# One load into 128 partitions in place of two into 64, in the attention stage of an encoder block

## The reference

```python
# A: 8 query heads on 2 key heads of 64, rotary, window of 2 chunks of 64, a learned sink per head
scores = jnp.einsum('bnqkgd,bnskd->bnkgqs', qc, kb) * (HEAD_DIM ** -0.5)
...
# B: 8 heads of 64, own chunk and the 8 before it, learned relative bias
scores = jnp.einsum('bnqhd,bnshd->bnhqs', qc, kb) * (HEAD_DIM ** -0.5)
scores = scores + bias[None, None]
probs = jax.nn.softmax(scores, axis=-1)
out = jnp.einsum('bnhqs,bnshd->bnqhd', probs, vb)
```

## Time and profile before

| | us |
|---|---|
| median of three runs | 2660.44 (2657.34 to 2663.78) |
| the profiled execution | 2667.05, its span 2665.1 |
| attention stage in the profile | 855 to 1232 |
| TensorE busy in the whole span | 2340.2 (88%) |
| VectorE, ScalarE, GpSimd busy | 1274.5, 1021.4, 837.4 |
| moved by the DMA engines | 508.67 MB, mean 191 GB/s |

### The profile page before, as it was taken

One profiled execution on the slowest core, in us unless ns is written; L12 is line 12 of the kernel. 1 busy time (PEld: TensorE's weight loads), 2 busy tenths in 40 slices (PEclk: granted clock), 3 DMA queues, 4 the chain that ended last, 5 costly groups with the idle time before them and its releaser, 6 DMA issues. The chain is left out here.

```text
span 2665.1 us, 37120 instructions
## 1 busy us (share of the span) xinstructions
PE 2340.2 (88%) x12222; PEld 1989.5 (75%) x12223; DVE 1274.5 (48%) x1935; ACT 1021.4 (38%) x1761; POOL 837.4 (31%) x801
## 2 busy tenths in 40 slices
PE   3899998999997789893699999559999999999990
PEld 2688887788886678883699999448888888888870
DVE  7201111100000567774433333476865758797774
ACT  4211111111111567774221221144654646576653
POOL 4255665510000011111222222034433434354451
PEclk9999999999998899997899999669999999999995
DMA  4145566622112877754544443358877979799987
GB/s 151 56 147 161 196 197 191 186 99 71 71 63 84 200 190 173 188 130 134 183 147 148 149 141 121 128 187 282 309 251 217 318 237 335 244 369 328 318 265 270
DMA packets 231745, 508.67 MB, mean 191 GB/s; under 512 B 25457, under 2 KB 88305, under 8 KB 230513
## 3 DMA queue, kind: packets, MB, share of 16 engines
q1 hardware_dynamic: 158480, 341.95, 38.6%
q0 software_dynamic: 32032, 93.35, 14.1%
q10 hardware_dynamic: 41152, 72.37, 7.7%
HBM read 386.13 MB, written 121.44 MB: 190 GB/s over the span
## 5 line engine op out<-in xcount | busy, mean ns | idle before, releaser
L408 DVE TENSOR_TENSOR pj_w_lo<-pj_w_raw,pj_w_hi 128x1024 fp32r<-128x1024 f32 x38 | 53.9, 1420 | 619.6 <-ACT pj_w_hi L300 619.5
L459 PE MATMUL pj_bank<-pj_hT_hi,pj_w_hi 128*128 128x512 f32 x960 | 259.4, 392 | 9.1 <-DVE pj_f_lo L425 5.7
L300 ACT ACTIVATE pj_w_hi<-pj_w_raw 128x1024 fp32r<-128x1024 f32 x38 | 40.2, 1060 | 591.8 <-PE pj_bank L459 520.8
L459 PE MATMUL pj_bank<-pj_hT_lo,pj_w_hi 128*128 128x512 f32 x960 | 258.4, 391 | 0.0
L459 PE MATMUL pj_bank<-pj_hT_hi,pj_w_lo 128*128 128x512 f32 x960 | 258.4, 391 | 0.0
L1870 POOL TENSOR_TENSOR ex_wd_lo<-weights_raw_d,ex_wd_hi 128x1024 fp32r<-128x1024 f32 x64 | 191.5, 3013 | 131.3 <-ACT ex_wd_hi L1898 131.3
L459 PEld LDWEIGHTS pj_bank<-pj_hT_hi,pj_w_hi 128*128 128x128 f32 x960 | 181.9, 190 | 47.8 <-issue 6.1
L459 PEld LDWEIGHTS pj_bank<-pj_hT_hi,pj_w_lo 128*128 128x128 f32 x960 | 181.4, 189 | 37.9
L459 PEld LDWEIGHTS pj_bank<-pj_hT_lo,pj_w_hi 128*128 128x128 f32 x960 | 181.4, 189 | 37.8
L1476 PE MATMUL mg_y_ps<-mg_aT_hi,mg_w_hi 128*128 128x256 f32 x512 | 149.3, 292 | 56.3 <-DVE mg_aT_lo L1388 48.8
L1952 DVE TENSOR_TENSOR ex_wd_lo<-weights_raw_d,ex_wd_hi 128x1024 fp32r<-128x1024 f32 x64 | 163.7, 2597 | 10.5 <-ACT ex_wd_hi L1898 10.5
(11 more groups left out here) (273 smaller groups left out, 5745.2 us busy)
## 6 DMA issues: line engine op xcount, KB each, us to landing
weights_raw_g<-in_w_exp_gate_dram SPq DMA_DIRECT2D x128, 512.0 KB, 5.9
weights_raw_u<-in_w_exp_up_dram SPq DMA_DIRECT2D x128, 512.0 KB, 8.9
weights_raw_d<-in_w_exp_down_dram SPq DMA_DIRECT2D x128, 512.0 KB, 6.8
pj_w_raw<-in_w_feat_dram SPq DMA_DIRECT2D x38, 512.0 KB, 4.5
scratch_gates<-pj_f_hi ACTq DMA_DIRECT2D x32, 512.0 KB, 4.9
mg_g_in<-scratch_gates SPq DMA_DIRECT2D x128, 128.0 KB, 2.9
pj_x_in<-in_x_dram SPq DMA_DIRECT2D x16, 512.0 KB, 3.5
scratch_qk<-pj_f_hi ACTq DMA_DIRECT2D x16, 512.0 KB, 5.0
```

The costliest lines, as they stand in the source:

```text
L300: act.activation(w_hi[n % 2][:], w_raw[n % 2][:], ACT.Copy).then_inc(whi_done, 1)
L408: dve.tensor_tensor(w_lo[n % 2][:], w_raw[n % 2][:], w_hi[n % 2][:], ALU.subtract).then_inc(wlo_done, 1)
L459: last = pe.matmul(eight[4 * p + b][:], w[p][:, k * P:(k + 1) * P], h[:, k, b * NB:(b + 1) * NB], start=(k == 0 and n == 0), stop=(k == KD ...
```

## The change

Each pair of loads into the lower and the upper 64 partitions becomes one load into all 128. For `k_st` and `aq_st` the source pattern gets a first dimension over the two parts; for `q_hi`, `q_lo`, `ak_hi` and `ak_lo` it gets a first dimension of size 2 and step 0 (`broadcast_to`). The counts that TensorE waits for are halved. The bytes written are the same.

```diff
-        QK_LOADS = 6
+        QK_LOADS = 3
...
-                sp.dma_start(k_st[p][:DH, cols].bitcast(F32), qk[0, k, rows, cols]).then_inc(landed, 16)
-                sp.dma_start(k_st[p][DH:, cols].bitcast(F32), qk[1, k, rows, cols]).then_inc(landed, 16)
+                sp.dma_start(k_st[p][:, cols].bitcast(F32), qk[:, k, rows, cols]).then_inc(landed, 16)
                 for part, both in enumerate((q_hi, q_lo)):
-                    for low in range(2):
-                        sp.dma_start(both[p][low * DH:(low + 1) * DH, cols].bitcast(F32), qk[part, q, rows, cols]
-                                     ).then_inc(landed, 16)
+                    sp.dma_start(both[p][:, cols].bitcast(F32),
+                                 qk[part, q, rows, cols].unsqueeze(0).broadcast_to([2, DH, HALF])).then_inc(landed, 16)
...
                 for part, keys in enumerate((ak_hi, ak_lo)):
-                    for low in range(2):
-                        sp.dma_start(keys[low * DH:(low + 1) * DH, padded_cols].bitcast(F32), rot_k[part, rows, cols]
-                                     ).then_inc(ak_in[c], 16)
+                    sp.dma_start(keys[:, padded_cols].bitcast(F32),
+                                 rot_k[part, rows, cols].unsqueeze(0).broadcast_to([2, DH, K_COLS])).then_inc(ak_in[c], 16)
...
-                for part in range(2):
-                    sp.dma_start(aq_st[seg % 2][part * DH:(part + 1) * DH, :, :].bitcast(F32),
-                                 rot_q[part, g, :, first:first + SEG_WINDOWS, :, :].rearrange("d w h q -> d w (h q)")
-                                 ).then_inc(aq_in[seg % 2], 16)
+                sp.dma_start(aq_st[seg % 2][:].bitcast(F32).rearrange("p w n -> p (w n)"),
+                             rot_q[:, g, :, first:first + SEG_WINDOWS, :, :].rearrange("a d w h q -> a d (w h q)")
+                             ).then_inc(aq_in[seg % 2], 16)
...
-                    pe.wait_ge(ak_in[s % GROUP_STEPS // 4], 64 * (g + 1))
+                    pe.wait_ge(ak_in[s % GROUP_STEPS // 4], 32 * (g + 1))
...
-                    pe.wait_ge(aq_in[seg % 2], 32 * (seg // 2 + 1))
+                    pe.wait_ge(aq_in[seg % 2], 16 * (seg // 2 + 1))
```

## The result

The changed kernel takes 3180.35 us (median of four runs, 3178.94 to 3180.53), the kernel before 2659.77 us beside it: a ratio of 1.1947, 95% interval 1.193 to 1.1964, or 520.6 us more. Forecast were 3164 us, 3080 to 3340.

A forecast was written before the change was run, and what follows sets the result against it. TensorE's chain bounds the attention stage before; joined loads make two DMA engines the bound: 741 + 62 us work plus 3 + 25 + 50 idle, stage 881 instead of 377 us, so 2660.4 + 504 = 3164 us, range 3080 to 3340.

The forecast's parts named there:

- Two engines per joined load: Attention stage loads: a source pattern beginning with a dimension of 2 is served by 2 of 16 DMA engines.
- The rate of one engine: Joined loads: 25.4 GB/s per engine, so 10.3 us per 512 KB load and 741 us for all.
- The place of the waits: Attention stage: ScalarE's copy in head 0 waits over 100 us, later heads 20 to 40; reloads near 1075 and 1590 us.
- Store 0: First at_o_both store, on SP's queue: served behind the whole opening burst of loads, delaying head 0's copy some 130 us.
- The other transfers on the two engines: Attention stage: a sixteenth of the remaining 20.5 MB lies on each of the two engines, 62 us.
- The idle time of the two engines: Attention stage: 3 us at the start, some 25 us at heads' ends, 50 us in the tail.
- The tail: End of the attention stage, after head 7's last loads: 77 us with some 27 us of transfers, 50 us idle.
- (1): Joined loads: all 16 engines serve them; gain 5 to 18 us, 2648 us; chance 0.08.
- (2): Attention stage: two engines whose work never stops, stage 803 + 3 us, kernel 3089 us; chance 0.10.
- (3): Joined loads: two slower engines, at 20.8 GB/s 3328 us, chance 0.12; at 14.1 GB/s 3758 us, chance 0.08.

The follow-up runs named there:

- the keys: Only the k_st loads joined as in the change, all other loads kept in pairs, against the kernel before: 2813.6 us, ratio 1.0581.

## Why the prediction was right

- **Two engines per joined load: shown.** 2401 closing packets fewer where 2400 were to be expected, two per load in a stretch of 30 us, a DMA share of 0.13, and the whole loss gone when the 64 rows come first. What the prediction read from the closing packets of the earlier trace rows for a first dimension of 4 held for one of 2. One transfer into 128 partitions was faster than two halves only with the 64 rows first: 2645 us, against 3180 us with the 2 first and 2660 us in halves.
- **The rate of one engine: the upper end, and a little more.** 52 to 53 GB/s for two (52 in 1006 to 1036 us; in 890 to 940 us 2.63 MB, 53 GB/s at a share of 0.13), 26.3 for one, where 25.4 was taken. A load of 512 KB takes 524288 B / 53 GB/s = 9.9 us and not 10.3, one of ak 5.0 to 5.1: 64 x 9.9 + 81 = 715 us in place of 741.
- **The place of the waits: right in time, loose in size.** First scores near 890 us (887.9 in the trace), copy in head 0 near 1055 (1053.71), reloads near 1075 and 1590 (1064.93 and 1591.87). Store 0 did sit behind the burst, but in two places: SP's issues of the loads took up to 18.15 us each, so that it was issued only at 1036.4 us, and then it was about 14 us in the queue (GpSimd, which waits for its landing, goes on at 1050.73 us). The later heads' copy waits are 53 to 63 us each, where 20 to 40 were forecast.
- **The other transfers on the two engines: under-sized, 127 us where 62 were counted.** The sum left out GpSimd's adding stores. The DMA view of before, 855 to 1232 us, counts their queue in its share of the 16 engines, 11.0% of 377 us or 41 us for each:

```profile
q0 software_dynamic: 5077, 4.17, 11.0%
```

  In the changed kernel they are 45 us. The other 82 us are SP's own transfers, where the mean rate of the queue over the whole program, 20.8 GB/s, gave 62.
- **The idle time of the two engines: over-sized, about 51 us where 78 were counted.** The tail was to have 50 us of it; the last 65 us of the stage hold 17 to 25 in the cut by pieces. Moving the stores or adding buffers, which gave 45 and 49 us, takes away most of what idle time there is.
- **The total is in part luck.** Three errors stand in the sum, -26 us in the loads, +65 in the other transfers and -27 in the idle time. They leave 12, which is why 881 us of stage stood so near 893 and 504 us so near 513.6; the median moved by 520.6. The last two are estimates, good to some 20 us.
- **Rivals.** (1), all 16 engines, fell as an account of this kernel, and its price was right for the kernel that does it: 2648 us forecast, 2645.4 measured. (2), no idle time at all, fell: 806 us against 893. With eight buffers or moved stores its condition nearly holds, and the stage is still 845.8 or 842.4 us, because the work was more than the 803 us counted. (3), slower engines, fell by the 52 GB/s.
- **What the model missed.** The work per engine alone does not give the cost of a part of the change. For the keys 5 to 50 us were expected, and they cost 153: 120 us of the stage were idle time of the two engines, and their work was counted 55 us too low. In the full change less of the loss is idle time, since the work fills the stage.

## What to carry to other kernels

Look at the first dimension of a load's source pattern before its size. In these runs a dimension of 2 in front, be it two planes (2885 us with those alone) or a copy with step 0 (2982 us), left 2 of 16 engines; a dimension of 64 in front cost nothing (2645 us, before 2660), and it can be had where the order of the partitions is free, as under a contraction. In the profile the slow loads showed as a DMA share near 0.13 with nothing computing, and as 2 closing packets instead of 16. Here they first hurt the stores behind them in a shared queue, so the wait (460.3 us of ScalarE's copies, 42.7 us for q_lo) carried another tensor's name; before blaming that tensor, ask what the queue was given ahead of it. And when the work of a few DMA engines is added up, take every queue, also one that another engine issues: q0, left out here, was 45 us for each engine.

## What the runs showed of the hardware

- An issue on SP is not always the 0.6 us of the earlier trace rows. Behind joined loads in the changed kernel many took 9.7 to 18.15 us (851 to 1036 us): about the time that one or two loads of 512 KB need on their two engines, 9.9 us each. SP issues nothing else meanwhile, and the other 14 engines are idle (share 0.13 in 1006 to 1036 us). What SP waits for in such an issue no run shows.
- Pairs of 64-partition loads ran at 226 to 241 GB/s with all engines busy; with the 64 rows first, so that one transfer alternates its 64 rows over 128 partitions, the opening burst ran at 403 in 857 to 886 us, with the same rows of 4 KB.
- Two engines alone reached 26.3 GB/s each (53 GB/s in 890 to 940 us of the changed kernel), about the 25.4 of each of sixteen in the earlier trace rows. So an engine gained hardly anything here from the other 14 being idle.
